# Two stacked transformer blocks on one core: the recurrent chunks' products summed in PSUM, and the ends of two stages rearranged

## The chip, the cores and the metric

The kernel runs on one core of a Trainium2 chip. The metric is the device time of one execution in microseconds (us), the median over runs. A core has five engines that run their own instruction streams and meet only at semaphores: TensorE (PE, matrix products into PSUM), VectorE (DVE), ScalarE (ACT), GpSimd (POOL, which can read and write SBUF but not PSUM) and SyncE (SP, which only issues DMA here).

## The reference, cut to what matters

The input is one sequence of 1024 tokens, 1024 wide, in float32. Two transformer blocks follow each other. The first mixes a gated linear recurrence (4 heads of 128) with sliding-window attention; the second has full attention with 8 query heads and a pooling mixer. The recurrence, for the queries q, keys k, values v and gates of one chunk, is this:

```python
sqk = jnp.einsum('bhtd,bhsd->bhts', qc, kc) * jnp.exp(dmat - m_t[..., None])
num = jnp.einsum('bhts,bhsd->bhtd', sqk, vc) + \
    w_inter[..., None] * jnp.einsum('bhvk,bhtk->bhtv', C, qc)
den = jnp.sum(sqk, axis=-1) + w_inter * jnp.einsum('bhk,bhtk->bht', n, qc)
h = num / jnp.maximum(jnp.abs(den), jnp.exp(-m_t))[..., None]
...
C_new = decay[..., None, None] * C + jnp.einsum('bhsv,bhsk->bhvk', vc * ws[..., None], kc)
```

After it come a root-mean-square norm over the 128 values of a head and a gate. The second block ends with a gated feed-forward, `x + (silu(h @ w_gate) * (h @ w_up)) @ w_down`, and x is the output.

## The kernel before

Activations lie with features on the partitions and tokens along the free dimension. Every weight product is three fp32r products (high times high, low times high, high times low), so TensorE works through most of the program. The order on each engine is written out by hand; a wait is a count on a semaphore. Three places are touched.

**The recurrent chunks** (`chunk_pe`, `chunk_dve`, `chunk_act`, `chunk_pool`, `chunk_sp`). The kernel takes 8 chunks of 128 tokens, one after the other. For chunk c, `turn(c)` (L1318 to L1320, TensorE) turns keys and values to token-major and multiplies keys by queries. `exponents(c)` (L1381, VectorE) adds the causal mask to a row of gate terms, `exponentials(c)` (L1279, ScalarE) takes exp, `weigh(c)` (L1387, VectorE) multiplies by the scores. `outputs(c)` is two products per head, queries with the state (L1340) and weights with values (L1344), in two places of PSUM. `new_state(c)` (L1395) updates the state from `update(c)` (L1329). `numerators(c)` copies the second product to SBUF (L1406) and adds the first times a factor per token (L1410). `denominators(c)` (L1419 to L1424), `squares_of(c)` (L1285, ScalarE), `variance(c)` (L1430, L1432) and `rstd(c)` (L1292, L1294, ScalarE) make the factor by which `scale(c)` (L1437, L1439) multiplies the numerators. `turn_back(c)` (L1353, TensorE) turns the result, and `gated(c)` (L1445) multiplies it by the gate. The 129th column of values is ones, so a product's 129th column is the denominator. GpSimd multiplies values by their weights (`values(c)`, L1238) and the gate by its gain (`gains_of(c)`, L1244), and inside chunks 6 and 7 it splits the attention keys (`pool_key`, L1538). `tokens(c)` (L1272, L1273, ScalarE) copies keys and values from PSUM.

**The entry of the second attention** (`SecondInput`). Queries are normed, rotated by `rope` (L2864 to L2867, VectorE), split by `query_hi` (ScalarE, L2807) and `query_lo` (VectorE, L2872), stored to DRAM by SyncE (L904) and fetched again in pieces (L1650). The last pair of heads is prepared inside the attention's first units: a unit is one head's 1024 scores (L1761, L1762), their maximum (L1857), exp, GpSimd's scaling (L1738), the turn (L1788) and the split (L1884). Unit 6 is the first that needs the last pair.

**The last group of the second feed-forward, and the output**. `downs` runs over 8 tiles of 128 output features, each with 12 products for both halves of the tokens, and `add_down` (L2497) adds 1024 columns into x. Then a block of its own, "output", turns 8 blocks of 128 tokens (L3089), copies them (L3096, ScalarE) and stores 512 KB each (L3102).

## Time and profile before

| | us |
|---|---|
| median of 3 runs (2515.71 to 2519.67) | 2518.65 |
| the profiled execution's own time | 2518.89 |
| its span | 2517.1 |
| recurrent chunks, first turn to the attention's first product | 320.8 to 398.3 |
| second attention, first product to its unit 6 | 1469.2 to 1497.4 |
| after the last down product | 2501.5 to 2517.1 |

| engine | busy us | share |
|---|---|---|
| TensorE products | 2401.7 | 95% |
| VectorE | 1254.9 | 50% |
| ScalarE | 827.1 | 33% |
| GpSimd | 343.3 | 14% |

A row of the timeline gives the start in us from the span's start, the duration, the engine and line, the operation with the names of what it writes and reads, how many instructions are merged (x), and in brackets how long the engine had been idle and what released it. Duration runs until the result is written, so on one engine the next row may start before the one above has ended. TensorE's clock is given as a share of its full 2.4 GHz.

### The profile page before, as it was taken

What the parts mean: (1) busy time and instruction counts of PE and PEld (TensorE: products, weight loads), DVE (VectorE), ACT (ScalarE), POOL (GpSimd) and SP (SyncE); (2) the same over time, 40 slices, a digit from 0 to 9 for tenths busy, and PEclk for the clock granted to TensorE, in tenths of its full rate; (3) what the DMA queues carried; (4) which work ended last, traced back from release to release, by engine and by line L of the source; (5) the groups of instructions that cost most, each with busy time, mean ns of one, the idle gap of its engine ahead of it and who ended that gap; (6) DMA issues with size and microseconds to landing.
All of it is one profiled execution on the core that took longest, in us unless ns stands there. A gap on an engine that the chain in (4) does not pass through costs nothing. (4 is left out here: it accounts for less than half of the span.)

```text
span 2517.1 us, 28601 instructions
## 1 busy us (share of the span) xinstructions
PE 2401.7 (95%) x10896; PEld 1936.6 (77%) x10896; DVE 1254.9 (50%) x1517; ACT 827.1 (33%) x1231; POOL 343.3 (14%) x263
## 2 busy tenths in 40 slices
PE   6999978899999999999998979999999999999998
PEld 5788866686788888888876757767788888888887
DVE  6457266527644444544456469973533333333333
ACT  5232256635322222222234458872311111111111
POOL 1120024224000000000032536631000000000000
PEclk9999998999999999999998989999999999999999
DMA  8246512033111111111123220003121111111111
GB/s 321 76 134 213 163 59 67 9 117 101 59 42 50 50 50 48 44 50 50 46 97 130 68 83 18 25 1 117 42 59 51 44 43 46 50 50 50 50 50 67
DMA packets 189005, 181.92 MB, mean 72 GB/s; under 512 B 8365, under 2 KB 166909, under 8 KB 188417
## 3 DMA queue, kind: packets, MB, share of 16 engines
q1 hardware_dynamic: 186288, 173.37, 21.6%
q0 software_dynamic: 2176, 7.36, 0.9%
q8 instruction: 49, 0.80, 0.1%
q10 hardware_dynamic: 465, 0.17, 0.0%
q14 instruction: 27, 0.22, 0.0%
HBM read 152.55 MB, written 28.33 MB: 72 GB/s over the span
## 5 line engine op out<-in xcount | busy, mean ns | idle before, releaser
L294 PE MATMUL ps<-hhi,whi 128*128 128x512 f32 x1696 | 663.5, 391 | 4.4 <-DVE wlo L219 2.0
L295 PE MATMUL ps<-hlo,whi 128*128 128x512 f32 x1696 | 660.5, 389 | 0.0
L296 PE MATMUL ps<-hhi,wlo 128*128 128x512 f32 x1696 | 660.5, 389 | 0.0
L219 DVE TENSOR_TENSOR wlo<-raw,whi 128x1024 fp32r<-128x1024 f32 x178 | 226.4, 1274 | 388.7 <-ACT whi L214 388.6
L294 PEld LDWEIGHTS ps<-hhi,whi 128*128 128x128 f32 x1696 | 318.7, 188 | 72.7 <-DVE wlo L219 2.4
L295 PEld LDWEIGHTS ps<-hlo,whi 128*128 128x128 f32 x1696 | 318.7, 188 | 67.2 <-issue 1.2
L296 PEld LDWEIGHTS ps<-hhi,wlo 128*128 128x128 f32 x1696 | 318.7, 188 | 66.6
L214 ACT ACTIVATE whi<-raw 128x1024 fp32r<-128x1024 f32 x178 | 184.5, 1049 | 389.2 <-PE ps L2346 286.5
L2497 DVE TENSOR_TENSOR arena<-arena,ps 128x1024 f32<-128x1024 f32 x160 | 195.3, 1220 | 141.0 <-PE ps L2346 140.1
L2344 PE MATMUL ps<-hid_hi,whi 128*128 128x512 f32 x640 | 250.0, 391 | 0.0
L2345 PE MATMUL ps<-hid_lo,whi 128*128 128x512 f32 x640 | 249.2, 389 | 0.0
L2346 PE MATMUL ps<-hid_hi,wlo 128*128 128x512 f32 x640 | 249.0, 389 | 0.0
L758 POOL TENSOR_TENSOR cbuf<-cbuf 128x512 f32<-128x512 f32 (+1 forms) x54 | 80.0, 1489 | 896.7 <-ACT cbuf L745 893.8
L2461 DVE SCALAR_TENSOR_TENSOR cbuf<-ps,par,cbuf 128x1023 f32<-128x1023 f32 x44 | 56.4, 1282 | 226.5 <-ACT cbuf L2370 226.5
L1738 POOL TENSOR_TENSOR cbuf<-cbuf,attn_stats 128x1024 f32<-128x1024 f32 x80 | 151.7, 1896 | 103.7 <-DVE attn_stats L1877 103.6
L2344 PEld LDWEIGHTS ps<-hid_hi,whi 128*128 128x128 f32 x640 | 120.1, 188 | 28.2 <-DVE arena L2497 3.3
L2346 PEld LDWEIGHTS ps<-hid_hi,wlo 128*128 128x128 f32 x640 | 120.1, 188 | 25.2
L2345 PEld LDWEIGHTS ps<-hid_lo,whi 128*128 128x128 f32 x640 | 120.1, 188 | 24.7
L2370 ACT ACTIVATE cbuf<-ps,par 128x1024 f32<-128x1024 f32 x44 | 53.1, 1206 | 223.1 <-PE ps L296 220.8
L2474 DVE TENSOR_TENSOR cbuf<-ps,cbuf 128x1024 f32<-128x1024 f32 x22 | 26.9, 1225 | 175.2 <-PE ps L296 156.6
L2384 ACT ACTIVATE hid_hi<-cbuf 128x1024 fp32r<-128x1024 f32 x44 | 46.5, 1057 | 203.5 <-DVEq L2476 110.8
L1788 PE MATMUL ps<-identF,cbuf 128*128 128x128 f32 x640 | 92.2, 286 | 19.5 <-POOL cbuf L1738 16.3
(330 smaller groups left out, 3303.0 us busy)
## 6 DMA issues: line engine op xcount, KB each, us to landing
raw<-in_w_up SPq DMA_DIRECT2D x66, 512.0 KB, 3.6
raw<-in_w_down SPq DMA_DIRECT2D x44, 512.0 KB, 3.4
raw<-in_w_in SPq DMA_DIRECT2D x32, 512.0 KB, 5.1
arena<-in_w_ada SPq DMA_DIRECT2D x32, 512.0 KB, 4.9
raw<-in_w_gate SPq DMA_DIRECT2D x22, 512.0 KB, 3.6
raw<-in_w_out SPq DMA_DIRECT2D x16, 512.0 KB, 3.8
arena<-x_park SPq DMA_DIRECT2D x2, 4096.0 KB, 12.1
x_park<-arena SPq DMA_DIRECT2D x4, 2048.0 KB, 8.5
```

Of the source, the lines that this page charges most:

```text
L214: nc.scalar.activation(whi[:, w.off % RING, :], raw[:, w.off % RAW, :], ACT.Copy).then_inc(hi_done, 1)
L219: nc.vector.tensor_tensor(wlo[:, w.off % RING, :], raw[:, w.off % RAW, :], whi[:, w.off % RING, :].bitcast(F32), ALU.subtract).then_inc(lo ...
L294: nc.tensor.matmul(acc[:, tok], whi[:, s, ws], hhi[:, k, tok], start=(k == 0), stop=False)
L295: nc.tensor.matmul(acc[:, tok], whi[:, s, ws], hlo[:, k, tok], start=False, stop=False)
L296: mm = nc.tensor.matmul(acc[:, tok], wlo[:, s, ws], hhi[:, k, tok], start=False, stop=(k == DK - 1))
L758: nc.gpsimd.tensor_tensor(total, total, cbuf[:, self.slot(r, k), tok], ALU.add).then_inc(self.added[r], 1)
L1738: nc.gpsimd.tensor_tensor(p, p, st[:, sl, 16:16 + q].unsqueeze(2).to_broadcast([P, q, T // q]), ALU.mult).then_inc(S["scaled"], 1)
L1788: mm = nc.tensor.transpose(ps_t[:, (4 * h + k) * P:(4 * h + k + 1) * P], src, identF[:, :])
L2344: nc.tensor.matmul(o, whi[:, s, ws], hidhi[:, p, tok], start=(r == 0), stop=False)
L2345: nc.tensor.matmul(o, whi[:, s, ws], hidlo[:, p, tok], start=False, stop=False)
L2346: mm = nc.tensor.matmul(o, wlo[:, s, ws], hidhi[:, p, tok], start=False, stop=(r == 1))
L2497: nc.vector.tensor_tensor(y[:, fo, :], y[:, fo, :], down[fo % 2][:, :], ALU.add)\
```

## The change

In the chunks, `outputs(c)` now lets both products of a head sum in one place of PSUM. For that the queries are first multiplied by the state's factor, on GpSimd (`gained_queries`), from rows that are stored to DRAM as `gain_rows` and loaded to all partitions, one chunk at a time. Heads 0 to 2 stay in PSUM and are squared and scaled from there; head 3 is copied to SBUF (`last_of`). `numerators` and the state's zero fill go. `exponents` moves from VectorE to GpSimd. The state is kept in two buffers, the last chunk's state update and key copy are left out, and `pool_key` runs after all chunks. At the second attention's entry, `rope` of the last pair moves from unit 1 to before unit 0, `query_hi` from unit 2 to unit 0, and `query_lo` from unit 3 to unit 1. At the end, the last group of down products goes by token half, 16 pieces of 6 products with adds of 512 columns, and the turning, copying and storing of the first four blocks is put between the second half's pieces.

```diff
+                    sp.wait_ge(gains_stored, 16)
+                    for c in range(1, 4):
+                        gain_load(sp, c)
...
-            for n in range(1, 4):
-                query(n)
+            query(1)
+            query(2)
+            pool.wait_ge(g_act, 4)
+            pool.dma_start(gains_dram, row_w).then_inc(gains_stored, 16)
+            query(3)
...
+            def exponents(c):
+                pool.wait_ge(rows_in[c // 2], 16)
+                if c >= 2:
+                    pool.wait_ge(c_main, c - 1)
+                nc.gpsimd.tensor_tensor(weights_[c % 2], row_bc[:, :, tok(c)],
+                                        causal[:, :].unsqueeze(1).to_broadcast([P, ML_H, P]), ALU.add).then_inc(c_arg, 1)
+
+            def gained_queries(c):
+                pool.wait_ge(gains_in[c % 3], 16 * ((c - 1) // 3 + 1))
+                if c >= 3:
+                    pool.wait_ge(c_main, c - 1)
+                nc.gpsimd.tensor_tensor(gained[c % 2], qk[:, 0:ML_H, tok(c)], gain_rows[c % 3], ALU.mult).then_inc(c_gained, 1)
...
             for c in range(2, NB):
-                values(c)
-                if c >= NB - 2:
-                    pool.wait_ge(c_values, c + 1)
-                    keys.pool_key(pool, c - NB + 2)
-                gains_of(c)
+                if c + 1 < NB:
+                    exponents(c + 1)
+                if c < NB - 1:
+                    values(c)
+                if c + 1 < NB:
+                    gained_queries(c + 1)
+                gains_of(c - 1)
+            gains_of(NB - 1)
+            pool.wait_ge(c_gain, NB)
+            for g in range(2):
+                keys.pool_key(pool, g)
...
             def outputs(c):
-                if c:
-                    pe.wait_ge(c_state, c)
-                    pe.wait_ge(c_num, c)
-                else:
-                    pe.wait_ge(c_zero, 2)
-                for h in range(ML_H):
-                    nc.tensor.matmul(ps_heads[h][:, 1, :], qk[:, h, tok(c)], state[:, h, :], start=True, stop=True)
                 pe.wait_ge(c_weights, c + 1)
                 pe.wait_ge(c_tokens, c + 1)
+                pe.wait_ge(c_zero, 1)
+                if c:
+                    pe.wait_ge(c_gained, c)
+                    pe.wait_ge(c_state, c)
+                    pe.wait_ge(c_last, c)
+                if c >= 2:
+                    pe.wait_ge(c_scaled, c - 1)
                 for h in range(ML_H):
-                    mm = nc.tensor.matmul(ps_heads[h][:, 0, :], weights_[c % 2][:, h, :], value_tok[c % 2][:, h, :],
-                                          start=True, stop=True)
+                    mm = nc.tensor.matmul(main_of(c, h), weights_[c % 2][:, h, :], value_tok[c % 2][:, h, :],
+                                          start=True, stop=(c == 0))
+                    if c:
+                        mm = nc.tensor.matmul(main_of(c, h), gained[c % 2][:, h, :], state[c % 2][:, h, :],
+                                              start=False, stop=True)
...
             def pe(self, pe):
                 in_pe(pe)
                 self.last_turn = chunk_pe(pe, self.keys)
-                pe.wait_ge(c_num, NB)
+                pe.wait_ge(c_scaled, NB)
...
+            def last_of(c):
+                dve.wait_ge(c_main, c + 1)
+                nc.vector.tensor_copy(last_head[c % 2], ps_last).then_inc(c_last, 1)
...
+                for hs, d in parts:
+                    nc.vector.tensor_tensor(r[:, hs], d, low[:, hs], ALU.max).then_inc(c_den, 1)
+                for i, (hs, d) in enumerate(parts):
+                    dve.wait_ge(c_den, 5 * c + i + 1)
+                    nc.vector.scalar_tensor_tensor(out=r[:, hs], in0=d, scalar=-1.0, in1=r[:, hs], op0=ALU.mult,
+                                                   op1=ALU.max).then_inc(c_den, 1)
...
             def squares_of(c):
-                act.wait_ge(c_num, c + 1)
+                act.wait_ge(c_den, 5 * c + 4)
...
             def act_unit(self, act, e):
                 if e == 0:
                     act.wait_ge(q_lo, 3)
                     act.wait_ge(q_stored[2], 64)
-                if e == 2:
                     self.query_hi(act, 3)
...
                 self.keys.dve_keys(dve, 1)
+                self.rope(dve, 4)
...
             def dve_unit(self, dve, e):
                 if e == 1:
-                    self.rope(dve, 4)
-                if e == 3:
                     self.query_lo(dve, 3)
...
+                def last_products():
+                    ...
+                    for n in range(2 * DK):
+                        fo, tok, o = n % DK, half(n // DK), tail_bank(n)
+                        ...
+                        mm.then_inc(B["sum"], 1)
+                        if n == DK + 1:
+                            pe.wait_ge(up_free, u0 + 4 * groups)
+                            pe.wait_ge(B["added"], DK)
+                        if DK + 1 <= n < DK + 5:
+                            finish.pe(pe, n - DK - 1)
+                    pe.wait_ge(B["added"], 2 * DK)
+                    for b in range(NB // 2, NB):
+                        finish.pe(pe, b)
...
+            def act(self, act):
+                for b in range(NB):
+                    wide = slice(0, T) if b < NB // 2 else half(0)
+                    act.wait_ge(self.turned, b + 1)
+                    nc.scalar.activation(rows[:, b, wide], up[b % 2][:, wide], ACT.Copy).then_inc(self.copied, 1)
+
+            def dve(self, dve):
+                for b in range(NB // 2, NB):
+                    dve.wait_ge(self.turned, b + 1)
+                    nc.vector.tensor_copy(rows[:, b, half(1)], up[b % 2][:, half(1)]).then_inc(self.other, 1)
```

What VectorE is given for one middle chunk, from `weigh` on, before:

```order
L1387 TENSOR_TENSOR chunk_work<-chunk_work,ps 128x512
L1395 SCALAR_TENSOR_TENSOR chunk_work<-chunk_work,gateF,ps 128x129 x4
L1406 COPY chunk_work<-ps 128x258 x2
L1410 SCALAR_TENSOR_TENSOR chunk_work<-ps,gateF,chunk_work 128x129 x4
L1419 SCALAR_TENSOR_TENSOR chunk_work<-chunk_work 128x4
L1422 TENSOR_TENSOR chunk_work<-chunk_work,gateF 128x4
L1424 RECIPROCAL chunk_work<-chunk_work 128x4
L1437 TENSOR_TENSOR chunk_work<-chunk_work 128x4
L1439 TENSOR_TENSOR chunk_work<-chunk_work 128x4x128
L1381 TENSOR_TENSOR chunk_work<-arena,causal 128x512
L1430 TENSOR_TENSOR chunk_work<-chunk_work 128x4
```

The same chunk after it, right behind `weigh` (gateF holds the gate columns, ps is PSUM, chunk_work is SBUF):

```order
L1443 COPY chunk_work<-ps 128x129
L1464 TENSOR_TENSOR chunk_work<-ps,gateF 128x3
L1464 TENSOR_TENSOR chunk_work<-chunk_work,gateF 128x1
L1467 SCALAR_TENSOR_TENSOR chunk_work<-ps,chunk_work 128x3
L1467 SCALAR_TENSOR_TENSOR chunk_work<-chunk_work 128x1
L1470 RECIPROCAL chunk_work<-chunk_work 128x4
L1454 SCALAR_TENSOR_TENSOR chunk_work<-chunk_work,gateF,ps 128x129 x4
L1485 TENSOR_TENSOR chunk_work<-chunk_work 128x4
L1487 TENSOR_TENSOR chunk_work<-ps,chunk_work 128x384
L1489 TENSOR_SCALAR chunk_work<-chunk_work 128x128
L1476 TENSOR_TENSOR chunk_work<-chunk_work 128x4
```

The state's update has moved behind the denominators; six large operations and the exponents are gone, and four small ones stand where three stood.

What GpSimd is given for the last chunks before:

```order
L1238 TENSOR_TENSOR chunk_work<-chunk_work,gateF 128x516
L1244 TENSOR_TENSOR chunk_work<-chunk_work,par 128x512
L1238 TENSOR_TENSOR chunk_work<-chunk_work,gateF 128x516
L1538 TENSOR_TENSOR hlo<-cbuf,hlo 64x1024
L1244 TENSOR_TENSOR chunk_work<-chunk_work,par 128x512
L1238 TENSOR_TENSOR chunk_work<-chunk_work,gateF 128x516
L1538 TENSOR_TENSOR hlo<-cbuf,hlo 64x1024
L1244 TENSOR_TENSOR chunk_work<-chunk_work,par 128x512
```

And after it (L1269 is `exponents`, L1282 `values`, L1276 `gained_queries`, L1288 `gains_of`, L1584 `pool_key`):

```order
L1269 TENSOR_TENSOR chunk_work<-arena,causal 128x512
L1282 TENSOR_TENSOR chunk_work<-chunk_work,gateF 128x516
L1276 TENSOR_TENSOR lead_work<-arena 128x512
L1288 TENSOR_TENSOR chunk_work<-chunk_work,par 128x512 x3
L1584 TENSOR_TENSOR hlo<-cbuf,hlo 64x1024 x2
```

Each chunk now has four such operations in a row instead of two, and both key splits stand behind the last of them.

VectorE at the second attention's entry, before (from the key split on):

```order
L1549 TENSOR_TENSOR hlo<-arena,hlo 64x1024 x2
L1857 TENSOR_REDUCE attn_stats<-ps 128x1
L1861 TENSOR_SCALAR attn_stats<-attn_stats 128x1
L1554 TENSOR_TENSOR hlo<-ps,hlo 128x16x64
L1857 TENSOR_REDUCE attn_stats<-ps 128x1
L1861 TENSOR_SCALAR attn_stats<-attn_stats 128x1
L1877 RECIPROCAL attn_stats<-attn_stats 128x1 x2
L1857 TENSOR_REDUCE attn_stats<-ps 128x1
L1861 TENSOR_SCALAR attn_stats<-attn_stats 128x1
L1884 TENSOR_TENSOR hhi<-ps,hhi 128x4x128 x2
L2864 TENSOR_TENSOR ps<-ps,arena 128x1024
L2865 TENSOR_TENSOR arena<-arena 128x1024
```

And after it:

```order
L1595 TENSOR_TENSOR hlo<-arena,hlo 64x1024 x2
L2943 TENSOR_TENSOR ps<-ps,arena 128x1024
L2944 TENSOR_TENSOR arena<-arena 128x1024
L2946 TENSOR_TENSOR arena<-arena,ps 128x1024
L1903 TENSOR_REDUCE attn_stats<-ps 128x1
L1907 TENSOR_SCALAR attn_stats<-attn_stats 128x1
```

The three operations of `rope` now stand ahead of the first maximum; in their old place stands the one of `query_lo`.

## Rows read from the trace of the kernel before

**Rows 1.** The page's head.
```profile
span 2517.1 us, 28601 instructions
```

**Rows 2.** Windows: from:to width, then busy (count) of PE PEld DVE ACT POOL, clock, DMA share, GB/s.
```profile
335.00:372.00 37.00, 26.75 (x216) 24.55 (x216) 29.21 (x97) 23.56 (x84) 7.94 (x8) 1.00 0.10 29
...
373.00:398.30 25.30, 14.78 (x69) 13.77 (x69) 17.74 (x48) 7.40 (x36) 8.08 (x6) 0.54 0.13 41
```

**Rows 3.** Timeline (start, duration, engine, line), VectorE, one chunk and the next one's start.
```profile
347.01 0.69 DVE L1387 TENSOR_TENSOR chunk_work<-chunk_work,ps 128x512 f32<-128x512 f32 x1 [1.16 <-ACT chunk_work L1279]
...
348.65 0.76 DVE L1406 COPY chunk_work<-ps 128x258 f32<-128x258 f32 x2
...
349.32 1.12 DVE L1410 SCALAR_TENSOR_TENSOR chunk_work<-ps,gateF,chunk_work 128x129 f32<-128x129 f32 x4
...
350.47 0.17 DVE L1419 SCALAR_TENSOR_TENSOR chunk_work<-chunk_work 128x4 f32<-128x4 f32 x1
...
354.46 0.69 DVE L1387 TENSOR_TENSOR chunk_work<-chunk_work,ps 128x512 f32<-128x512 f32 x1 [1.16 <-ACT chunk_work L1279]
```

**Rows 4.** Timeline, ScalarE, the same chunk.
```profile
350.47 0.31 ACT L1285 ACTIVATE chunk_work<-chunk_work 128x128 f32<-128x128 f32 x1 [2.55 <-DVE chunk_work L1410]
...
353.17 1.26 ACT L1279 ACTIVATE chunk_work<-chunk_work,gateF 128x128 f32<-128x128 f32 x4
```

**Rows 5.** Timeline, VectorE, operations with both inputs in SBUF beside GpSimd.
```profile
357.93 0.24 DVE L1419 SCALAR_TENSOR_TENSOR chunk_work<-chunk_work 128x4 f32<-128x4 f32 x1
...
373.64 2.11 DVE L1437 TENSOR_TENSOR chunk_work<-chunk_work 128x4 f32<-128x4 f32 x1
...
384.04 1.62 DVE L1419 SCALAR_TENSOR_TENSOR chunk_work<-chunk_work 128x4 f32<-128x4 f32 x1
```

**Rows 6.** Timeline, GpSimd, what ran there at those moments.
```profile
357.10 1.05 POOL L1238 TENSOR_TENSOR chunk_work<-chunk_work,gateF 128x516 f32<-128x516 f32 x1
...
373.37 2.35 POOL L1538 TENSOR_TENSOR hlo<-cbuf,hlo 64x1024 fp32r<-64x1024 f32 x1
...
383.29 2.35 POOL L1538 TENSOR_TENSOR hlo<-cbuf,hlo 64x1024 fp32r<-64x1024 f32 x1
```

**Rows 7.** Timeline, TensorE, query products of two chunks at either clock.
```profile
359.90 1.06 PE L1340 MATMUL ps<-chunk_work,arena 128*128 128x129 f32 x8
...
377.44 1.93 PE L1340 MATMUL ps<-chunk_work,arena 128*128 128x129 f32 x8
```

**Rows 8.** Timeline, VectorE, entry of the second attention.
```profile
1463.36 2.46 DVE L1549 TENSOR_TENSOR hlo<-arena,hlo 64x1024 fp32r<-64x1024 f32 x2
...
1470.28 1.23 DVE L1857 TENSOR_REDUCE attn_stats<-ps 128x1 f32<-128x1024 f32 x1 [4.45 <-PE ps L1762]
...
1480.48 1.22 DVE L2864 TENSOR_TENSOR ps<-ps,arena 128x1024 f32<-128x1024 f32 x1
...
1489.33 2.12 DVE L2872 TENSOR_TENSOR arena<-arena,cbuf 128x1024 fp32r<-128x1024 f32 x1
```

**Rows 9.** Timeline, SyncE's queue, entry of the second attention.
```profile
1491.47 1.21 SPq L904 DMA_DIRECT2D query_parts<-arena  x2
```

**Rows 10.** Timeline, TensorE, entry of the second attention.
```profile
1490.42 1.09 PE L1788 MATMUL ps<-identF,cbuf 128*128 128x128 f32 x8 [2.13 <-POOL cbuf L1738]
...
1497.43 0.79 PE L1761 MATMUL ps<-hlo,gateR 128*128 128x512 f32 x1 [5.92 <-DMA gateR<-query_parts]
...
1505.89 1.04 PE L1788 MATMUL ps<-identF,cbuf 128*128 128x128 f32 x8
```

**Rows 11.** Timeline and one window, the program's last 15 us.
```profile
2501.58 1.22 DVE L2497 TENSOR_TENSOR arena<-arena,ps 128x1024 f32<-128x1024 f32 x1 [1.50 <-PE ps L2346]
...
2505.30 2.01 PE L3089 MATMUL ps<-identF,arena 128*128 128x128 f32 x16 [0.24 <-ACT arena L3096]
...
2510.84 1.94 ACT L3096 ACTIVATE arena<-ps 128x1024 f32<-128x1024 f32 x2 [0.27 <-PE ps L3089]
...
2514.00:2515.00 1.00, 0.00 (x0) 0.00 (x0) 0.00 (x0) 0.00 (x0) 0.00 (x0) 1.00 1.00 410
```

More of the change, by code:

```diff
@@ L1210, in block_kernel @@
         c_main, c_update, c_out = (sem("chunk_" + x) for x in ("outputs", "update", "out_turned"))
-        c_state, c_zero, c_num, c_den, c_sq, c_var, c_log, c_rstd, c_scaled, c_done = (
-            sem("chunk_" + x) for x in ("state", "zero", "numerators", "den", "squares", "var", "logs", "rstd", "scaled",
-                                        "done"))
+        c_state, c_zero, c_last, c_den, c_sq, c_var, c_log, c_rstd, c_scaled, c_done, c_gained = (
+            sem("chunk_" + x) for x in ("state", "ones", "last_head", "den", "squares", "var", "logs", "rstd", "scaled",
+                                        "done", "gained"))
         def tok(c):
@@ L1393, in new_state @@
                     dve.wait_ge(c_state, c)
-                for h in range(ML_H):
-                    ins = nc.vector.scalar_tensor_tensor(out=state[:, h, :], in0=state[:, h, :],
-                                                         scalar=decay[:, h, c:c + 1], in1=ps_heads[h][:, 2, :],
-                                                         op0=ALU.mult, op1=ALU.add)
+                    for h in range(ML_H):
+                        ins = nc.vector.scalar_tensor_tensor(out=new[:, h, :], in0=old[:, h, :],
+                                                             scalar=decay[:, h, c:c + 1], in1=update_of(h),
+                                                             op0=ALU.mult, op1=ALU.add)
@@ L1455, in chunk_dve @@
                     weigh(c + 1)
-                new_state(c)
-                numerators(c)
+                last_of(c)
                 denominators(c)
+                if c + 1 < NB:
+                    new_state(c)
                 if c:
                     scale(c - 1)
-                if c + 2 < NB:
-                    exponents(c + 2)
                 variance(c)
@@ L2532, in last @@
                     else:
-                        add_down(At(groups - 1), last_tiles())
+                        for n in range(2 * DK):
+                            tail_add(dve, n)
+                        finish.dve(dve)
                 def tail_operands():
@@ L3055, in block_kernel, with __init__, pe, sp @@
         out2.first_added = sem("w_out_2_first_added")
-        ffn2 = feed_forward("ffn2", T_FF2, xt, False, out2, norm2_2)
+        rows = chunk_work[:, :].rearrange("p (b d) -> p b d", d=D)
+        out_v = out[0].rearrange("(b p) d -> b p d", p=P)
+        class Output:
+            def __init__(self):
+                self.turned, self.copied, self.stored = sem("out_turned"), sem("out_copied"), sem("out_stored")
+                self.other = sem("out_other_half")
+            def pe(self, pe, b):
+                if b >= 2:
+                    pe.wait_ge(self.copied, b - 1)
+                if b >= NB // 2 + 2:
+                    pe.wait_ge(self.other, b - NB // 2 - 1)
+                for k in range(DK):
+                    mm = nc.tensor.transpose(up[b % 2][:, k * P:(k + 1) * P], xt[:, k, b * P:(b + 1) * P], identF[:, :])
+                mm.then_inc(self.turned, 1)
+            def act(self, act):
[7 more added lines that the diff above has]
+                    nc.vector.tensor_copy(rows[:, b, half(1)], up[b % 2][:, half(1)]).then_inc(self.other, 1)
+            def sp(self, sp):
+                for b in range(NB):
+                    sp.wait_ge(self.copied, b + 1)
+                    if b >= NB // 2:
+                        sp.wait_ge(self.other, b - NB // 2 + 1)
+                    sp.dma_start(out_v[b], rows[:, b, :]).then_inc(self.stored, 16)
+                sp.wait_ge(self.stored, 16 * NB)
+        ffn2 = feed_forward("ffn2", T_FF2, xt, False, out2, norm2_2, finish=Output())
         with nc.Block("ffn2") as block:
```

156 lines of the change are left out of this document (78 added, 78 removed).

## The prediction

> **What bounds the kernel now.** I read the page's head first, then the busy time of each engine by stretch, and after that only the three stretches that the change touches. TensorE is 95% busy over the span, so what can be won is where it waits. The timeline of each engine in the chunks comes next: it shows a cycle that repeats to a few hundredths, and the reader is to follow who releases whom. The last views are the timelines of the second attention's entry and of the program's end. All sums are made against the profiled execution, 2518.89 us with a span of 2517.1 [rows 1]; it stands 0.2 us above the median of the runs, 2518.65, so the forecast for the one is that for the other.
>
> In the middle of the chunks TensorE is busy for 26.75 of 37 us at full clock, VectorE for 29.2 [rows 2]; no engine is full, so a chain of waits sets the period. One period is 354.46 - 347.01 = 7.45 us [rows 3]. Its chain: `weigh` and the state update 1.64 (347.01 to 348.65), copies 0.67, numerators 1.15 (to 350.47) [rows 3]; ScalarE then takes 2.70 for squares, token copies and rstd (350.47 to 353.17) and 1.29 for the exponentials (to 354.46) [rows 3, 4]. That is 7.45, all of it. TensorE fills its gaps inside this. In the last 25.3 us the clock is 0.54 of full and TensorE does 14.8 us of work [rows 2].
>
> **Part 1, the chunks.** From the chain go the copies of four heads, the numerators and, since it now stands behind the denominators, the state: 1.04 + 0.67 + 1.15 = 2.86 (the state's 1.04 is 1.64 less the 0.60 of `weigh`). Added are the copy of one head, a quarter of the copies' 0.67 and about 0.3 with its semaphore, and the denominators, which squares did not wait for before: four small operations in two dependent pairs, about 0.5 by the 0.17 of the small one in the chain [rows 3]. Unhindered, the period would be 7.45 - 2.86 + 0.8 = 5.4 us. TensorE's busy time per period is 26.75 / 37 x 7.45 = 5.4 as well [rows 2], so it could not go lower.
>
> But it is hindered. A VectorE operation with both inputs in SBUF that starts while GpSimd works ends only when GpSimd does. The small one at 357.93 took 0.24 and ended at 358.17, GpSimd's at 358.15; that at 373.64 took 2.11 and ended at 375.75, GpSimd's at 375.72; that at 384.04 took 1.62 and ended at 385.66, GpSimd's at 385.64 [rows 5, 6]. The change gives GpSimd four operations of 1.0 us per chunk where there were two [rows 6], and the first, `exponents`, waits for the same signal of `outputs` as VectorE's `last_of`. So they start together, and VectorE's denominators of head 3, two operations with both inputs in SBUF, fall into the burst: the first waits for what is left of GpSimd's first operation, about 0.5, the second for GpSimd's second, about 0.9; the factor of `scale` meets the fourth, about 0.7. Walk the period again: `weigh` 0.6, head copy 0.3, denominators 0.5 + 1.4, reciprocal and state 1.15, wait 0.6, scale of PSUM and one head 0.75, variance 0.3, rstd 0.45, exponentials 1.3 = 7.3 us. That is 0.15 less than now. I take 7.3; the ends are 5.4 (no stall) and 9.1 (VectorE passed over for the whole burst of four, 4.0 in place of the 2.1 of stalls, behind `weigh` and copy).
>
> The Trainium skill, page "SBUF — State Buffer", section "Who interferes with whom", says that VectorE and GpSimd share one pair of ports, that a VectorE instruction with two SBUF inputs needs it against a GpSimd instruction that reads SBUF, and that who comes first holds it for the whole instruction. The three pairs of rows agree. By that rule alone the stalls are the ones I count; had the page been wrong, the period would be 5.4 and the kernel about 14 us faster than I say. The same section lets a `tensor_scalar` contend too, which no row here shows; it would add up to 0.9 per chunk for head 3's scaling where that meets a GpSimd operation.
>
> Gains outside the period: the first chunk has no state product and two copies for a state update, 0.8. The key split inside chunk 6 now costs VectorE 2.11 for an operation that takes under 0.2, so 2.0 in the loop [rows 5]; it moves behind the last chunk. There both splits (2.35 each [rows 6]) run in a row and hit the last denominators and the last factor, so 2 x 2.1 come back; against them go the last `update` (2.0 at the low clock, by 1.93 for eight products [rows 7]), the last state (1.0), copies and numerators (1.8) and the stall of 1.62 - 0.17 = 1.45 that is there now [rows 5]. The attention's first product now waits for `scale` of the last chunk, not for the numerators: squares, rstd and scale, about 3, of which TensorE's turning of values at the low clock hides about 1.5. Tail: -6.3 + 4.2 + 1.5 = -0.6, and I take -1.2, since the turn back before it comes earlier too. Sum for the chunks: six periods x 0.15 = 0.9, + 0.8 + 2.0 + 1.2 = 4.9 us gained. The added DMA (256 KB per chunk, ordered a chunk ahead) has 7 us per chunk on queues that are 10% busy [rows 2] and costs nothing; if it came late it would delay `outputs` directly.
>
> **Part 2, the second attention's entry.** VectorE is free from 1465.8 (1463.36 + 2.46) to 1470.28 [rows 8]. `rope`, three operations of 1.2 starting at 1465.8, ends at 1469.4 and is hidden. In unit 1, at 1480.48, `query_lo` (1.2, and about 0.5 of stall beside GpSimd) takes the place of 3.5 us of `rope`. The low parts are then ready at 1482.2. They were ready, and were sent, at 1491.47 [rows 9], and unit 6 began at 1497.43 after TensorE had waited 5.92 for that fetch [rows 10]: 5.96 from send to use. Now 1482.2 + 5.96 = 1488.2. What is late next: the turn of unit 3, at 1490.42 [rows 10], which comes 1.9 earlier since VectorE saves 1.8 in unit 1, at 1488.5; TensorE ends it at 1489.5 and unit 6 starts at once. That is 7.9 earlier. The pipeline behind it also does not run empty: units follow every 2.75 us, so unit 6's turn, now at 1505.89 [rows 10], comes at 1488.5 + 3 x 2.3 = 1495.4 with three units between, where the first of them has its exponentials ready. 10.5 earlier at most; I take 9.5, bounds 3.5 (only `rope`'s time) and 11.
>
> **Part 3, the end.** Now: the last add starts at 2501.58, eight blocks are turned and copied until 2512.78, and the stores keep all 16 DMA engines busy at 410 GB/s [rows 11] until a microsecond before the end. The work added ahead of the last product is four blocks of eight transposes, 0.9 each (16 in 2.01 [rows 11]): 3.5. Then a half-wide add 0.7, four blocks 3.6, half-wide copy 0.8, to 2501.5 + 8.6 = 2510.2, 2.6 earlier. By the DMA: the first store of the four is ordered at 2507.5, 2 MB at 410 GB/s is 5.1, and with 0.8 before and 0.9 behind, the end is at 2514.3, 2.8 earlier. I take 2.7, bounds 1.5 and 3.5.
>
> **Sum.** 4.9 + 9.5 + 2.7 = 17.1. 2518.9 - 17.1 = 2501.8, say 2502.
>
> **Rivals.**
> A, no stall that matters: GpSimd's operations slip between VectorE's, as in the middle chunks where they cost 0.07. For it: the stalls seen are short wherever GpSimd's operation was nearly over. Against: both now start from one signal. Period 5.4: seven times 1.9 more, 2518.9 - 17.1 - 13.3 = 2488.5.
> B, the second attention gains only what `rope` cost there, 3.5, since another wait stands right behind the fetch (scaling on GpSimd, which also has the pooling work). The fetch wait of 5.92 speaks against it. 2518.9 - 11.1 = 2508.
> C, the other side: GpSimd's four operations overlap by 0.05 at their seams, and VectorE, which waits, is not let in between. Then its denominators wait for all four and the period is 9.1; TensorE idles about 4 us in each and its clock goes to 1.2 GHz as it did at 377.44, where eight products took 1.93 and not 1.06 [rows 7]. Its work per chunk becomes 5.0 x 1.9 = 9.5 and with the waits the period about 12. At full clock: chunks lose 6 x 1.65 less the 4.0 of the other terms = 6 us, total 2518.9 + 6 - 12.2 = 2513. At the low clock: 6 x 4.7 less 4.0 less about 4 for a tail that is at the low clock either way = 20 lost, total 2518.9 + 20 - 12.2 = 2527, slower. It decides when the clock falls by the third chunk. No back-to-back pair in the trace had a VectorE operation waiting across its seam, so nothing excludes it.
>
> **How the numbers follow.** Forecast 0.66 (2502, own range 2496 to 2509), A 0.08 (2488), B 0.14 (2508), C at full clock 0.06 (2513), C at the low clock 0.06 (2527). The range 2492 to 2512 leaves out A and C. No change means within 0.2%, 5 us, which is about what a measurement of this kernel can tell: above 2513.6 lie the low-clock case and half of the full-clock one. Faster 0.89, same 0.05, slower 0.06.
>
> **What would show it.** In the changed kernel's timeline: the small operation on head 3 (the 128x1 ones) takes 0.5 to 1.0 and ends with a GpSimd operation; `weigh` to `weigh` is about 7.3; both key splits stand behind the last chunk beside long small VectorE operations. Unit 6 of the second attention starts at once behind a turn, with no DMA as its releaser. The last store is ordered about 8.8 us after the last down product. The forecast is wrong if the period is under 6.5 or over 8, if TensorE's clock falls before the sixth chunk, or if TensorE still waits for the fetch.

## The result, and the profile after

The changed kernel took 2502.98 us, the median of 4 runs (2501.87 to 2504.64), beside 2519.03 for the kernel before. The ratio is 0.9937, its 95% interval 0.9922 to 0.9952: 16 us gained where 17.1 were forecast. Run once more against the kernel before, its ratio was 0.9930 (0.9917 to 0.9944). The profiled execution has a span of 2501.4 us; [rows 1] has 2517.1.

The span is best cut where the change begins and ends. The stretches are: start to the first `weigh`; to the attention's first product (the chunks); to the next weight product (the first attention); to the key split of the second attention; to the last product of its output projection (the second attention with its entry); to the first product of the last down group; to the end.

| stretch | before | after | difference | forecast |
|---|---|---|---|---|
| start to first `weigh` | 325.59 | 322.63 | -2.96 | 0 |
| chunks | 72.70 | 66.40 | -6.30 | -4.9 |
| first attention | 79.49 | 82.44 | +2.95 | 0 |
| to the key split | 985.58 | 987.20 | +1.62 | 0 |
| second attention | 352.34 | 343.83 | -8.51 | -9.5 |
| to the last down group | 642.20 | 642.10 | -0.10 | 0 |
| last group and output | 59.20 | 56.79 | -2.41 | -2.7 |

The three places gained 17.2 where 17.1 were forecast, but by misses that cancel: the chunks gave 1.4 more, the entry 1.0 less, the end 0.3 less. What lies outside them gave 1.5 back. These are the windows of the kernel before, then of the changed one, for the two stretches that moved without being touched (first attention, and the one behind it); columns as in [rows 2].

```profile
398.29:477.78 79.49, 66.50 (x390) 50.38 (x389) 52.42 (x119) 63.77 (x212) 34.83 (x24) 0.97 0.16 47
...
477.78:1463.36 985.58, 964.78 (x4103) 774.08 (x4104) 489.76 (x465) 304.72 (x342) 109.34 (x82) 0.99 0.21 66
```

```profile
389.03:471.47 82.44, 67.24 (x390) 52.20 (x389) 52.35 (x118) 63.91 (x212) 34.81 (x24) 0.93 0.16 45
...
471.47:1458.67 987.20, 964.57 (x4103) 773.74 (x4104) 489.68 (x465) 304.73 (x342) 109.35 (x82) 0.99 0.21 66
```

In the first attention TensorE's granted clock is 0.93 after and 0.97 before; it is busy 0.74 us longer and idle 2.2 longer. Most of that arises by the second unit's turn. That turn, and one score product just before it, in the kernel before and then in the changed one:

```profile
410.26 0.28 PE L1774 MATMUL ps<-hlo,query_operand 128*128 128x256 f32 x1
...
411.21 1.04 PE L1788 MATMUL ps<-identF,cbuf 128*128 128x128 f32 x8
```

```profile
402.20 0.41 PE L1822 MATMUL ps<-hlo,query_operand 128*128 128x256 f32 x1
...
404.12 1.47 PE L1834 MATMUL ps<-identF,cbuf 128*128 128x128 f32 x8
```

The turn comes 12.9 us behind the stage's start before (411.21 - 398.29) and 15.1 after (404.12 - 389.03); the product takes 0.28 at full clock and 0.41 at half.

One chunk of the changed kernel, on VectorE (the answer to [rows 3]):

```profile
342.43 0.69 DVE L1439 TENSOR_TENSOR chunk_work<-chunk_work,ps 128x512 f32<-128x512 f32 x1 [0.55 <-ACT chunk_work L1334]
...
343.43 0.94 DVE L1464 TENSOR_TENSOR chunk_work<-chunk_work,gateF 128x1 f32<-128x1 f32 x1
...
344.40 0.97 DVE L1467 SCALAR_TENSOR_TENSOR chunk_work<-chunk_work 128x1 f32<-128x1 f32 x1
...
345.50 1.12 DVE L1454 SCALAR_TENSOR_TENSOR chunk_work<-chunk_work,gateF,ps 128x129 f32<-128x129 f32 x4
...
346.54 0.16 DVE L1485 TENSOR_TENSOR chunk_work<-chunk_work 128x4 f32<-128x4 f32 x1
...
347.20 0.48 DVE L1489 TENSOR_SCALAR chunk_work<-chunk_work 128x128 f32<-128x128 f32 x1
...
347.79 0.17 DVE L1478 TENSOR_TENSOR chunk_work<-chunk_work 128x4 f32<-128x4 f32 x1
...
349.73 0.69 DVE L1439 TENSOR_TENSOR chunk_work<-chunk_work,ps 128x512 f32<-128x512 f32 x1 [0.56 <-ACT chunk_work L1334]
```

and on GpSimd beside it (L1269 `exponents`, L1282 `values`, L1276 `gained_queries`, L1288 `gains_of`):

```profile
343.08 1.27 POOL L1269 TENSOR_TENSOR chunk_work<-arena,causal 128x512 f32<-128x512 f32 x1 [2.78 <-PE ps L1403]
...
344.31 1.05 POOL L1282 TENSOR_TENSOR chunk_work<-chunk_work,gateF 128x516 f32<-128x516 f32 x1
...
345.31 1.27 POOL L1276 TENSOR_TENSOR lead_work<-arena 128x512 f32<-128x512 f32 x1
...
346.54 1.06 POOL L1288 TENSOR_TENSOR chunk_work<-chunk_work,par 128x512 f32<-128x512 f32 x1
```

From `weigh` to `weigh` it is 349.73 - 342.43 = 7.30 us, the 7.3 of the forecast. Read the ends: the 128x1 operation at 343.43 ends at 344.37, GpSimd's `exponents` at 344.35; the one at 344.40 ends at 345.37, `values` at 345.36. Both are stalls: the operation is done only when GpSimd's is. VectorE is let in at each seam, that is where GpSimd goes from one operation to the next. The burst now is 343.08 to 347.60, 4.5 us.

The tail, on VectorE, GpSimd and TensorE:

```profile
381.64 2.10 DVE L1485 TENSOR_TENSOR chunk_work<-chunk_work 128x4 f32<-128x4 f32 x1
...
384.25 1.97 DVE L1489 TENSOR_SCALAR chunk_work<-chunk_work 128x128 f32<-128x128 f32 x1
...
381.38 4.75 POOL L1584 TENSOR_TENSOR hlo<-cbuf,hlo 64x1024 fp32r<-64x1024 f32 x2
...
386.27 1.11 PE L1412 MATMUL ps<-identF,chunk_work 128*128 128x128 f32 x4 [6.03 <-DVE chunk_work L1489]
```

The two key splits hold VectorE for 2.10 (the factor) and 1.97 (the scaling of head 3); TensorE waits 6.03 for the second of these.

The entry of the second attention (the answer to [rows 8 to 10]): `rope`, `query_lo`, the store of the low parts, then TensorE's turn of unit 3, the scores of unit 6 and its turn.

```profile
1461.17 1.23 DVE L2943 TENSOR_TENSOR ps<-ps,arena 128x1024 f32<-128x1024 f32 x1
...
1475.08 1.47 DVE L2951 TENSOR_TENSOR arena<-arena,cbuf 128x1024 fp32r<-128x1024 f32 x1
...
1476.58 1.21 SPq L906 DMA_DIRECT2D query_parts<-arena  x2
...
1483.63 1.97 PE L1834 MATMUL ps<-identF,cbuf 128*128 128x128 f32 x8 [2.14 <-POOL cbuf L1784]
...
1485.26 0.78 PE L1807 MATMUL ps<-hlo,gateR 128*128 128x512 f32 x1
...
1492.54 1.03 PE L1834 MATMUL ps<-identF,cbuf 128*128 128x128 f32 x8
```

Unit 6 starts at 1485.26 right behind a turn, without a wait. Counted from the key split it is 26.6 us, before 34.1 (1497.43 - 1463.36, [rows 8, 10]): 7.5 earlier, 7.9 forecast. Unit 3's turn starts 25.0 behind the split, before 27.1, so it comes 2.1 earlier for the 1.9 of the sum; but it falls into a spell at 1.2 GHz and takes 1.97, where the sum had 1.0. Unit 6's turn is 33.9 behind the split, before 42.5: 8.7 earlier.

The end (the answer to [rows 11]): last add, last turning, last copy, and the stores' window.

```profile
2491.95 0.69 DVE L2247 TENSOR_TENSOR arena<-arena,ps 128x512 f32<-128x512 f32 x1 [0.67 <-PE ps L2344]
...
2492.69 3.91 PE L3149 MATMUL ps<-identF,arena 128*128 128x128 f32 x32 [0.78 <-DVE arena L2247]
...
2496.64 0.60 ACT L3156 ACTIVATE chunk_work<-ps 128x512 f32<-128x512 f32 x1 [0.28 <-PE ps L3149]
```

```profile
2496.00:2500.00 4.00, 0.60 (x6) 0.36 (x4) 1.14 (x2) 0.96 (x2) 0.00 (x0) 1.00 1.01 415
```

The DMA engines are at work until about a microsecond before the end (2501.4) here as well.

### The profile page after: what moved, and what is told of

It is laid out like the page before. It is cut to its first block and busy times, and to the rows that moved or that the text cites. A ratio compares the mean times of both kernels' runs of the same rounds, so it can differ in the third digit from the quotient of the medians.

```text
span 2501.4 us, 28585 instructions
## 1 busy us (share of the span) xinstructions
PE 2393.0 (96%) x10880; PEld 1930.9 (77%) x10880; DVE 1251.9 (50%) x1498; ACT 825.1 (33%) x1230; POOL 361.9 (14%) x278
## 5 line engine op out<-in xcount | busy, mean ns | idle before, releaser
L296 PEld LDWEIGHTS ps<-hhi,wlo 128*128 128x128 f32 x1696 | 318.4, 188 | 66.4
L2575 DVE TENSOR_TENSOR arena<-arena,ps 128x1024 f32<-128x1024 f32 x152 | 185.5, 1220 | 129.0 <-PE ps L2422 128.1
L2420 PE MATMUL ps<-hid_hi,whi 128*128 128x512 f32 x608 | 237.5, 391 | 0.0
L2421 PE MATMUL ps<-hid_lo,whi 128*128 128x512 f32 x608 | 236.7, 389 | 0.0
L2422 PE MATMUL ps<-hid_hi,wlo 128*128 128x512 f32 x608 | 236.6, 389 | 0.0
L2420 PEld LDWEIGHTS ps<-hid_hi,whi 128*128 128x128 f32 x608 | 114.1, 188 | 26.8 <-DVE arena L2575 3.2
L2422 PEld LDWEIGHTS ps<-hid_hi,wlo 128*128 128x128 f32 x608 | 114.2, 188 | 23.9
L2421 PEld LDWEIGHTS ps<-hid_lo,whi 128*128 128x128 f32 x608 | 114.2, 188 | 23.4
```

The source lines that it names most:

```text
L296: mm = nc.tensor.matmul(acc[:, tok], wlo[:, s, ws], hhi[:, k, tok], start=False, stop=(k == DK - 1))
L2420: nc.tensor.matmul(o, whi[:, s, ws], hidhi[:, p, tok], start=(r == 0), stop=False)
L2421: nc.tensor.matmul(o, whi[:, s, ws], hidlo[:, p, tok], start=False, stop=False)
L2422: mm = nc.tensor.matmul(o, wlo[:, s, ws], hidhi[:, p, tok], start=False, stop=(r == 1))
L2575: nc.vector.tensor_tensor(y[:, fo, :], y[:, fo, :], down[fo % 2][:, :], ALU.add)\
```

## The experiments

Each kernel was profiled once and, but for one, timed against the kernel before in 3 or 5 rounds. "The stretch" of the chunks is the one of the table above. This is what they gave:

| kernel | median us | ratio to before (95%) | `weigh` to `weigh` | chunks' stretch |
|---|---|---|---|---|
| chunks_alone | 2515.58 | 0.9984 (0.9975 to 0.9993) | 7.30 | 66.8 |
| entry_alone | 2509.28 | 0.9964 (0.9950 to 0.9978) | 7.45 | 72.3 |
| end_alone | 2518.57 | 1.0000 (0.9991 to 1.0009) | 7.5 | 72.4 |
| den_from_psum | 2496.79 | 0.9912 (0.9897 to 0.9927) | 6.4, 7.1 | 60.6 |
| retimed_burst_alone | 2496.75 | 0.9909 (0.9893 to 0.9926) | 6.98 | 64.2 |
| retimed_and_den_psum | 2493.49 | 0.9896 (0.9879 to 0.9913) | 5.7 | 57.6 |
| retimed_keys_in_loop | 2488.03 | 0.9872 (0.9856 to 0.9889) | 5.7 | 54.9 |
| retimed_keys_order | 2492.75 | 0.9889 (0.9872 to 0.9905) | 5.5 to 6.5 | 58.3 |
| early_scale | 2496.09 | 0.9904 (0.9889 to 0.9920) | 6.7 to 8.0 | 60.9 |
| after_again | 2503.81 | 0.9930 (0.9917 to 0.9944) | 7.30 | 65.3 |
| before_again | 2519.90 (one run) | | 7.45 | 72.8 |

### Each part alone: chunks_alone, entry_alone, end_alone

The kernel before with one part of the diff each.

> The kernel before with the chunks' part of the change alone. By the parts theory (three parts that add up, each worth what its own stretch shows in the profile): from the first weigh to the attention's first product 66.4 us as in the full change (72.7 before), 6.3 us gained there, and 6.3 give or take 2 in the whole, the 2 for where the spells of low TensorE clock fall behind it. By the prediction's own sum 4.9. By the rival that the gain of the chunks is given back in the first attention (its first product came 9.3 us earlier, the feed-forward behind it only 4.7): 2 to 3 us gained.

> The kernel before with rope, query_hi and query_lo of the last pair moved, nothing else. Parts theory: 8.6 us gained between the key split and the last turn of the second attention, and as much in the whole; unit 6 starts behind unit 3's turn with no DMA as its releaser. The prediction had 9.5. Rival B: only rope's own 3.5 us, another wait takes the fetch's place.

> The kernel before with the last group of down products by token half and the output put between them, nothing else. Parts theory: 2.4 us gained from the start of the last down group to the end, and in the whole. The prediction had 2.7. Rival: the first 8 half-wide pieces, with the adds between, cost TensorE what the stores win, 1 us or less.

The entry gives 9 us in the whole (0.36% of 2519.8; 5.5 to 12.6), which rejects rival B's 3.5. In its own stretch it is 343.2 us; the kernels with the old entry have 352.3, 353.9, 353.9 and 354.1. The chunks give 4.0 (1.8 to 6.3) where their stretch gives 5.9: the first attention has 82.3 us here too, as in the changed kernel, and 79.5 and 79.3 in the two profiles of the kernel before. The 4.0 exclude neither of the two forecasts, 6.3 and 2 to 3. The end's stretch is 56.65, 2.55 less than before, as forecast, but the whole shows nothing: 1.0000, within 2.3 us either way. Its window:

```profile
2460.10:2516.75 56.65, 51.16 (x257) 42.60 (x255) 28.18 (x32) 9.45 (x11) 0.00 (x0) 0.99 0.18 74
```

So the stretch is shown and the gain in the whole isn't: the interval just about holds it. The three ratios add up to 13 us (4.0 + 9.1 + 0.0), each uncertain by 2.3 or more, and the full change gave 16 and 17.6; they don't contradict each other, nor can they place 3 us.

### The port: den_from_psum

```diff
-                parts = (..., (slice(3, 4), last_head[c % 2][:, P:VA]))
+                parts = (..., (slice(3, 4), ps_last[:, P:VA]))
```

> The changed kernel, with head 3's denominator read from PSUM and not from its copy in SBUF: neither of its two small operations has two SBUF inputs any more. Port theory (a VectorE operation with both inputs in SBUF waits for GpSimd's running one): both 128x1 operations fall from 0.94 and 0.97 to under 0.2. Inside it, two forecasts of the time: (a) the stalls were on the chain and simply go, period 7.3 to 5.7, 10 us less than the changed kernel in all (about 2493); (b) the burst of four GpSimd operations is still there, and the factor of scale and the two operations of variance, which now come 1.7 earlier, fall into it: they end with GpSimd's second, third and fourth operation, period 7.0, 2 us less (about 2501). I hold (b). Rival: no port, the two were slow for their semaphores: they stay at 0.9 and the time at 2503.

VectorE's denominators, variance, and GpSimd's fourth operation in one chunk:

```profile
349.61 0.23 DVE L1464 TENSOR_TENSOR chunk_work<-ps,gateF 128x3 f32<-128x3 f32 x2
...
349.80 0.22 DVE L1467 SCALAR_TENSOR_TENSOR chunk_work<-ps,chunk_work 128x3 f32<-128x3 f32 x2
...
352.79 1.01 DVE L1476 TENSOR_TENSOR chunk_work<-chunk_work 128x4 f32<-128x4 f32 x1
...
352.74 1.04 POOL L1288 TENSOR_TENSOR chunk_work<-chunk_work,par 128x512 f32<-128x512 f32 x1
```

Each row merges two operations, on heads 0 to 2 and on head 3. Head 3's, which took 0.94 and 0.97 with the copy, are now done together with their partners in 0.23 and 0.22: the same operation, the same GpSimd burst, one input less from SBUF. That is the port, and rules out the semaphores. The variance now pays 1.01, ending at 353.80 with GpSimd's at 353.78. Neither of my two forecasts of the time held. The stalls moved, as (b) says: the factor takes 0.76 and 0.39 in turn for its 0.16, and the variance pays in every second chunk only. The loop's gaps alternate between 6.4 and 7.1, since after a long one GpSimd's burst starts ahead of `weigh` (342.05 and 342.31), and is over by the variance; after a short one it starts behind it (349.29 and 348.68). It is 6.2 us less than the changed kernel, between (a)'s 10 and (b)'s 2. 2.2 of the stretch's 5.8 are in the tail, which neither counted.

### GpSimd's burst moved: the two retimed kernels

```diff
...
-            for c in range(2, NB):
+            for c in range(1, NB):
                 if c + 1 < NB:
                     exponents(c + 1)
-                if c < NB - 1:
-                    values(c)
+                pool.wait_ge(c_var, 2 * c)
+                if c + 1 < NB - 1:
+                    values(c + 1)
                 if c + 1 < NB:
                     gained_queries(c + 1)
...
                 gains_of(c - 1)
...
```

> The changed kernel; GpSimd's order alone is changed: exponents still start with outputs, but values (one chunk further ahead), gained_queries and gains_of wait until VectorE has made the variance. Port theory: only one GpSimd operation is left beside VectorE's small ones, so the first 128x1 operation keeps its 0.94 and the second falls to under 0.2; factor and variance run free. Period 7.3 - 0.85 = 6.45, total about 2503 - 6 = 2497, tail unchanged. Rival (TensorE or ScalarE sets the period, the stalls lie beside it): the stalls go and the period stays at 7.3.

> As before this, and head 3's denominator read from PSUM. Port theory: no VectorE operation of the chunks' loop meets a GpSimd one while it has two SBUF inputs. Period 0.6 + 0.3 + 0.45 + 1.1 + 0.16 + 0.95 + 0.35 + 0.45 + 1.3 = 5.7, 1.0 less than with the denominators alone (6.73), 7 us in all: about 2490. Rival: GpSimd now becomes late itself, since its three operations start only behind the variance (gained queries or gate gains are waited for), and the period stays at 6.5 or above, 2495.

With the burst moved alone the period is 6.98, not 6.45. These rows of it show the second 128x1 operation and GpSimd's `exponents`:

```profile
350.48 0.45 DVE L1463 TENSOR_TENSOR chunk_work<-chunk_work,gateF 128x1 f32<-128x1 f32 x1
...
350.96 1.19 DVE L1466 SCALAR_TENSOR_TENSOR chunk_work<-chunk_work 128x1 f32<-128x1 f32 x1
...
350.87 1.26 POOL L1269 TENSOR_TENSOR chunk_work<-arena,causal 128x512 f32<-128x512 f32 x1
```

The moved burst reaches the next chunk's denominators: the first operation takes 0.45 and ends with `gains_of`, the second takes 1.19 and ends at 352.15, `exponents` at 352.13. The forecast of 2497 came true by luck: the stretch gave 2.2 only, and the untouched ones behind it the rest (80.2 and 983.8, where the changed kernel has 82.4 and 987.2). With both edits the period is 5.66 to 5.75, as forecast (5.7), and the time 2493.5 (2490 forecast).

### The key splits back in the loop: retimed_keys_in_loop

```diff
+                if c == NB - 2:
+                    pool.wait_ge(c_gained, NB - 1)
+                    keys.pool_key(pool, 0)
+                if c == NB - 1:
+                    pool.wait_ge(c_gain, NB - 2)
+                    keys.pool_key(pool, 1)
                 gains_of(c - 1)
...
-            for g in range(2):
-                keys.pool_key(pool, g)
```

> As the last, and the two key splits in the last two rounds of GpSimd's loop, behind the variance, where GpSimd has no values to make. Behind the last chunk no key split runs beside VectorE: its tensor_scalar and variance, 1.97 and 2.25 with the denominators alone, take 0.3 and 0.16. 4 us come off the tail, of which the low clock there may take 1: 2487. Rival: the second key split moves into the last chunk's factor or variance instead, 2 us there: 2489.

This is the fastest, 2488.0: 32 us under the kernel before (0.9872 of 2520.5) and 15 under the change. One chunk, from `weigh` to `weigh`, then the last chunk's scaling and variance:

```profile
341.17 0.69 DVE L1442 TENSOR_TENSOR chunk_work<-chunk_work,ps 128x512 f32<-128x512 f32 x1 [1.17 <-ACT chunk_work L1337]
...
342.09 0.23 DVE L1467 TENSOR_TENSOR chunk_work<-ps,gateF 128x3 f32<-128x3 f32 x2
...
344.70 0.16 DVE L1479 TENSOR_TENSOR chunk_work<-chunk_work 128x4 f32<-128x4 f32 x1
...
346.83 0.69 DVE L1442 TENSOR_TENSOR chunk_work<-chunk_work,ps 128x512 f32<-128x512 f32 x1 [0.51 <-ACT chunk_work L1337]
...
374.08 0.28 DVE L1492 TENSOR_SCALAR chunk_work<-chunk_work 128x128 f32<-128x128 f32 x1
...
374.80 0.16 DVE L1481 TENSOR_TENSOR chunk_work<-chunk_work 128x4 f32<-128x4 f32 x1
```

From this chunk on no operation is held for long (the factor, L1488, still pays 0.15 to 0.25 at the end of `exponents`, and once 0.45 at that of `gains_of`). TensorE nearly bounds the loop: it is busy for 5.2 of the 5.7. The tail is 2.4 shorter than with the splits behind the loop (13.2 for 15.6).

### Two orders on VectorE that fail: retimed_keys_order, early_scale

```diff
+                variance(c)
                 if c:
                     scale(c - 1)
-                variance(c)
-                if c:
                     gated(c - 1)
```

and, in early_scale, from the same place to the head of the loop:

```diff
+                if c:
+                    scale(c - 1)
                 if c + 1 < NB:
                     weigh(c + 1)
...
                     new_state(c)
-                if c:
-                    scale(c - 1)
                 variance(c)
```

> As the last, and on VectorE the variance of a chunk ahead of the scaling of the chunk before. rstd then waits for ScalarE's own token copies and not for VectorE: 0.4 off the period of 5.7, unless TensorE's 5.4 of work per period is the floor. I expect 5.5, 1.5 us in all: 2485.5. Rival: the later scaling delays the turn back and outputs, which waits for it, and the period is longer than 5.7: 2489.

> The version with the retimed burst, the denominator from PSUM and the key splits in the loop (2488.0), and on VectorE the scaling of the chunk before moved ahead of weigh, where VectorE waits for the exponentials. The scaling's 0.95 leaves the way from the denominators to the variance; weigh comes 0.3 later. Period: TensorE's 5.4 of work, 5.5 in place of 5.7. In the tail TensorE does not wait 3.5 us for the scaling of chunk 5 before the last outputs: these end about 2 to 3 us earlier. Together 1.2 + 2.5: about 2484.5. Rival: as with the variance moved ahead (2492.8), what is won on VectorE comes back as a wait of TensorE or of the first operation on head 3's copy, and the time is 2488 or more.

Both are slower than 2488.0, by 4.7 and 8.1. In the first, the last four gaps between `weigh`s add up to 1.0 more (23.8 for 22.8), as the rival has it, the first three to 0.9 less; the tail is 3.3 longer (16.5 for 13.2). TensorE waits there for the scaling before it can turn back: 9.3 us in four waits, longest 5.0, where retimed_keys_in_loop has 5.4 in two. The longest begins with the port again. The key split waits for the variance, which now comes ahead of the scaling, and so head 3's scaling meets it:

```profile
372.59 1.91 DVE L1492 TENSOR_SCALAR chunk_work<-chunk_work 128x128 f32<-128x128 f32 x1
...
372.07 2.34 POOL L1586 TENSOR_TENSOR hlo<-cbuf,hlo 64x1024 fp32r<-64x1024 f32 x1 [1.57 <-DVE chunk_work L1481]
```

It takes 1.91 for the 0.28 that it takes alone. (The profiled execution of this kernel, 2497.66, is the slowest of its four.) The second puts the factor where the moved burst is. Its VectorE and GpSimd:

```profile
348.23 1.27 DVE L1488 TENSOR_TENSOR chunk_work<-chunk_work 128x4 f32<-128x4 f32 x1
...
350.48 0.67 DVE L1442 TENSOR_TENSOR chunk_work<-chunk_work,ps 128x512 f32<-128x512 f32 x1
...
348.21 1.27 POOL L1276 TENSOR_TENSOR lead_work<-arena 128x512 f32<-128x512 f32 x1
```

The factor, 0.16 where it runs free (346.54 in the changed kernel), takes 1.27 and ends at 349.50 with `gained_queries` at 349.48, and `weigh`, the head of the chain, comes that much later. From first to last `weigh` this kernel takes 50.1 us for 41.7. Its tail did get shorter as expected (10.9 for 13.2), which the loop outweighs. The same small operation costs nothing or a whole GpSimd operation, by its place alone.

### The same programs once more: before_again, after_again

> The kernel before, unchanged, one more profiled execution. The question is the stretches that the change does not touch. If the low-clock spells lie at the same places in each execution of one program, they lie here as in the first profile: none near 1675, one of 3.4 us at 148, and 79.5 us between the first attention's first product and the next weight products. If they differ between executions, the untouched stretches differ by up to 2 us each, by 1.7 for each spell of 3.4 us more or less, and a single profile can't place a gain of 2 us.

> The changed kernel, unchanged. As before_again: the same spells (396.1 to 402.9 in the first attention, 467.7 to 474.6) and 82.4 us for the first attention if the program sets them, others if the execution does. Chunks 66.4, second attention's entry 343.8 from key split to the next weight products' end, last group to the end 56.8, each within 0.3, since these are chains of waits. Ratio to the kernel before 0.9937 again, within 0.001.

The windows around 148 us, of the changed kernel's first and second profile:

```profile
144.00:153.00 9.00, 9.00 (x67) 7.84 (x67) 7.34 (x6) 2.24 (x3) 0.00 (x0) 1.00 0.39 120
```

```profile
144.00:153.00 9.00, 9.00 (x54) 7.25 (x53) 7.34 (x6) 2.22 (x3) 0.00 (x0) 0.69 0.43 145
```

Same program, same products, a granted clock of 1.00 and of 0.69. In the second the first `weigh` comes at 326.57, later than in the kernel before; in the first at 322.63. So a difference ahead of the chunks can be the clock's alone. That holds for only a part of the 2.96 us. The rest is there already at a product far ahead of them, here in the kernel before and in the changed one:

```profile
47.82 0.76 PE L363 MATMUL ps<-hhi,whi 128*128 128x512 f32 x1 [6.08 <-DVE hlo L512]
```

```profile
46.10 0.77 PE L363 MATMUL ps<-hhi,whi 128*128 128x512 f32 x1 [4.95 <-DVE hlo L512]
```

This product starts at 47.1 to 47.9 in the four profiles with the old chunks and at 45.9 to 46.6 in all nine with the new ones, with the same operations in the same order up to it. So about 1.4 us of the gain (46.2 for 47.6 in the mean) go with the changed program and not with the single execution, and no forecast had them; why they arise is open.

The kernel before repeated its stretches within 0.3 us except the second attention (353.9 for 352.3, with a low clock near 1680 that the first profile didn't have). The stretch from the first attention to the key split is 985.6 and 985.4 there, but 987.2 in entry_alone and end_alone too, so the 1.62 that it seems to lose comes without the new chunks too. The changed kernel's chunks came out at 65.3 for 66.4, and its first attention at 80.9 for 82.4, the spell there being 3.4 us long and not 6.8. My bound of 0.3 for the chunks was too narrow: from first to last `weigh` they agree (49.0 and 48.9), but the tail took 17.4 and 16.3.

## Why the prediction was right, step by step

- **The period, 7.3.** Measured 7.30, by terms that were off both ways, so that it agrees this closely is luck. Assumed 0.5 + 1.4 for the denominators, measured 2.05 with their stalls (343.35 to 345.40); assumed 1.0 for each GpSimd operation, measured 1.27 for two of the four and 1.05 for the others. The stall of 0.7 in the factor, which the walk has as "wait 0.6", didn't come (0.16 at 346.54, exactly at the seam to the fourth operation); factor and scaling together took 1.07 for 0.75. The mechanism was right: one SBUF input less took both stalls away.
- **`tensor_scalar`, the rule that no row showed.** The Trainium skill, page "SBUF — State Buffer", section "Who interferes with whom", lets it contend as well. Here it took 1.97 beside the key split, 0.48 in the changed kernel's loop (0.34 to 0.84 in the loops of the others) and 0.28 alone: the trace agrees, and it is 0.2 per chunk, not the 0.9 set as its limit.
- **First chunk, key split, tail: 0.8, 2.0, 1.2.** The gaps between the eight `weigh`s shrank by 1.6 in the first three, 0.6 in the next three and 2.3 in the last, the tail by 1.8: 6.3 together, for 4.9. So what came out is 1.4 more than the sum. Behind the last chunk the two splits cost 3.6 (2.10 - 0.16 and 1.97 - 0.28) for the 4.2 assumed; they hit the factor and head 3's scaling, not the denominators.
- **The second attention's entry, 9.5.** Unit 6 came 7.5 earlier for 7.9, its turn 8.7 for the 9.5 to 10.5, the stretch 8.5 for the 9.5 taken. The term that was too large is the way from unit 3's turn to unit 6's: 3 x 2.3 = 6.9 assumed, 8.9 measured (1492.54 - 1483.63): two steps of 2.7, and 3.4 for the first, whose turn ran at the low clock. Against the three profiles with the old entry that have a low clock near 1680 in this stretch, it is 10. Rival B (3.5) is rejected by the ratio of the edit alone.
- **The end, 2.7.** The stretch gave 2.4 to 2.55 in every profile. The last store is ordered 5.5 us behind the last down product (2497.4 and 2491.9) and not 8.8 behind it as "what would show it" says: the 8.8 holds from where that product stood before the blocks were put between (2444.6 + 43.7 = 2488.3, 9.1 before 2497.4). The sum used the right one, the sentence was wrong. In the whole this part is not resolved.
- **Rival A** (no stall) is what retimed_and_den_psum measures: its period is 5.7 where A had 5.4, and it is 9.5 us faster than the change, for A's 13.3. **Rival C** did not occur: VectorE got in at every seam, and the clock stayed at 2.4 GHz from the second chunk to 372 us.
- **The added wait and DMA** cost nothing that shows: TensorE has no wait for the gain rows.
- **What the prediction left out** is that a stretch that isn't touched can move by 3 us. The total came out at 16 for 17.1 since the 2.96 ahead of the chunks and the 4.5 behind them nearly cancelled, and since the misses of the three parts did: that part of the agreement is luck.

Open: why the program's first 47 us are about 1.4 us shorter with the new chunks, and why the first attention loses 0.5 to 3 us when the changed chunks stand ahead of it. In all three profiles with them unaltered it has 80.9 to 82.4 (79.3 to 80.4 in the four with the old chunks), and the low clock falls on its busy start. That the arrival time sets where the low clock falls is likely by these, but the two profiles of one program differ as well, so it isn't shown.

## What to carry to other kernels

Before moving work to GpSimd, list VectorE's operations with two SBUF inputs (and its `tensor_scalar`) that can start while it runs: each ended here when GpSimd's current operation did, however small it was. Read one input from PSUM where it still lies there, and start GpSimd's burst behind the last of these operations; here both together took the period from 7.30 to 5.7, either alone to 7.0 or 6.4 to 7.1. Compare two profiles by stretches cut at the edits, and take a second profile of the same program before believing 3 us in a stretch that the edit doesn't touch.

## What the runs showed of the hardware

- GpSimd's 128x512 operation took 1.27 us with two inputs read in full (or one repeated over the heads) and 1.05 where the second input is one value per 128 elements.
- VectorE is let in between two GpSimd operations that follow each other without a gap, at every seam seen; a stalled operation's end lies 0.01 to 0.03 us behind GpSimd's where it has 1 or 4 columns, and 0.08 to 0.09 behind it for the 128x128 `tensor_scalar`.
- The spells at 1.2 GHz between long stretches at 2.4 GHz fell at other places in two executions of one program (none and 6.8 us near 148), with TensorE busy without a gap there. Three profiles with one of 3.4 us near 1680 took 1.6 to 1.8 us longer in the second attention than the one without (353.9 to 354.1 for 352.3), with the same entry.
